# Spreading a block's recurrence, norm and queries over 122 slots, and its closing norm between the dots

## The reference

```
proj = h @ w_in                                  # 1024 -> conv group and RWKV-7 group
y_rw = RWKV-7 recurrence per head, group norm, + bonus, * gate
mix  = concat(y_cv, y_rw) @ w_o
h1   = layer_norm(ALPHA * h + mix)
q    = (h1 @ w_q)            # 8 heads x 2 halves x 128
sc   = q . sub_keys          # 16 times 128 scores a token
s_top, i_top = top_k(sc, 16)
best, pos = top_k(s_top0[:, None] + s_top1[None, :], 16)   # 16 of 256 pairs, per head
idx = i_top0 * 128 + i_top1 at pos;  gate = softmax(best)
hu  = peer_u[idx] . h1       # 128 rows of 1024 numbers for each token
out = sum(gelu(hu) * gate * peer_v[idx])
h2  = layer_norm(ALPHA * h1 + out)
```

## Time and profile before

| | |
|---|---|
| median of 3 runs | 3719.94 us (3712.74 to 3723.7) |
| the profiled execution | 3718.71 us, its span 3717.0 us |
| busy: PE, DVE, ACT, POOL | 3218.4, 2426.5, 801.9, 2105.5 us |
| granted TensorE clock, mean | 0.945 |
| DMA | 1239.85 MB |
| first dot of block 0 / block 1 / block 7 | at 672.08, 1058.31, 3297.66 us |

### The profile page before, as it was taken

How to read it: one execution, slowest core, us unless ns; L and a number is a source line. 1 busy time by engine, 2 the same in 40 slices (tenths; PEclk the granted TensorE clock), 3 DMA queues, 4 the chain that set the end, 5 groups by cost and what they waited for, 6 DMA issues and landing times.

```text
span 3717.0 us, 58838 instructions
## 1 busy us (share of the span) xinstructions
PE 3218.4 (87%) x17619; PEld 1706.6 (46%) x17619; DVE 2426.5 (65%) x5758; ACT 801.9 (22%) x1946; POOL 2105.5 (57%) x2172
## 2 busy tenths in 40 slices
PE   4996898599879987998799879987998799888977
PEld 3663565444534453445344534443444344442532
DVE  5463523867676767676766676667666766686795
ACT  2331000122122212221222122212221222121121
POOL 0012700377567756775677567756775677566575
PEclk9997999799999999999899989999999999999989
DMA  4344211899999999999999999999999999999997
GB/s 158 92 127 120 87 33 43 303 406 400 353 405 408 401 353 403 408 401 355 402 408 396 347 398 408 402 354 395 408 404 359 393 408 406 362 372 399 377 387 300
DMA packets 395698, 1239.85 MB, mean 334 GB/s; under 512 B 50834, under 2 KB 98326, under 8 KB 395216
## 3 DMA queue, kind: packets, MB, share of 16 engines
q0 software_dynamic: 302112, 1099.09, 76.4%
q1 hardware_dynamic: 91504, 134.41, 10.5%
q10 hardware_dynamic: 1728, 2.16, 0.2%
HBM read 1212.00 MB, written 31.94 MB: 335 GB/s over the span
## 4 chain that ended last, share of the span: by engine, by line
PE 58%; DVE 17%; issue 10%; DMA 4%; ACT 1%; DVEq 1%; POOL 0%; SPq 0%; ACTq 0%; POOLq 0%
PE ep_ps L1247 36%; PE front_ps L1116 9%; PE ep_ps L1293 5%; DVE rings L1630 4%; PE front_ps L1167 3%; PE front_ps L1185 3%; DMA rings<-in_peer_v_dram,idx 3%; DVE top_places L1544 1%; DVE top_places L1547 1%; DVE others L1545 1%; DMA rings<-in_peer_u_dram,idx 1%; DVE top_val L1546 1%; ACT diag L1366 1%; DVE top_idx L1548 1%; DVE top_val L1543 0%
## 5 line engine op out<-in xcount | busy, mean ns | idle before, releaser
L1247 PE MATMUL ep_ps<-rings,diag 128*128 128x512 f32 x4096 | 2027.6, 625 | 342.1 <-ACT diag L1366 296.1
L584 POOL DMA_INDIRECT rings<-in_peer_u_dram,idx x1024 | 985.3, 962 | 872.1 <-DVE hu L1630 318.0
L1630 DVE CUSTOM_DVE_ANT_0 rings<-rings,x_ps 128x1024 f32<-128x1024 f32 x1024 | 1237.4, 1212 | 89.8 <-DMA rings<-in_peer_u_dram,idx 54.3
L1247 PEld LDWEIGHTS ep_ps<-rings,diag 128*128 128x128 f32 x4096 | 736.9, 196 | 1110.7 <-issue 720.6
L584 POOL DMA_INDIRECT rings<-in_peer_v_dram,idx x1024 | 983.3, 960 | 386.8 <-issue 259.2
L1366 ACT ACTIVATE diag<-ident,act_v 128x128 f32<-128x128 f32 x1024 | 349.7, 391 | 262.0 <-PE ep_ps L1247 178.2
L1185 PEld LDWEIGHTS front_ps<-h1T,wq_ring 128*128 128x128 f32 x2304 | 284.1, 196 | 55.6 <-issue 54.9
L1185 PE MATMUL front_ps<-h1T,wq_ring 128*128 128x128 f32 (+1 forms) x2304 | 285.9, 276 | 1.2 <-issue 1.2
L348 PE MATMUL job_ps<-rings,w_ring 128*128 128x352 f32 (+2 forms) x672 | 208.7, 473 | 7.9 <-DMA w_ring<-in_w_in_dram 4.0
L1293 PE MATMUL ep_ps<-rings 128*128 128x352 f32 x576 | 197.2, 482 | 1.3 <-DMA rings<-in_w_in_dram 1.3
L1350 ACT ACTIVATE q_T<-front_ps 128x128 f32<-128x128 f32 (+1 forms) x144 | 38.4, 267 | 604.1 <-PE front_ps L1185 604.1
(11 more groups left out here) (349 smaller groups left out, 2903.8 us busy)
## 6 DMA issues: line engine op xcount, KB each, us to landing
wq_ring<-scratch_wq_tiles SPq DMA_DIRECT2D x144, 512.0 KB, 7.1
rings<-in_peer_u_dram,idx POOLq DMA_INDIRECT x1024
rings<-in_peer_v_dram,idx POOLq DMA_INDIRECT x1024
ops<-scratch_op_blocks SPq DMA_DIRECT2D x35, 256.0 KB
scratch_wq_tiles<-in_w_q_dram SPq DMA_DIRECT2D x16, 512.0 KB, 5.1
w_ring<-in_w_in_dram SPq DMA_DIRECT2D x12, 512.0 KB, 3.9
rings<-in_w_in_dram SPq DMA_DIRECT2D x12, 512.0 KB, 4.4
xrow<-in_x_prompt_dram SPq DMA_DIRECT2D x8, 512.0 KB, 3.7
```

What stands on the lines that cost most here:

```text
L584: return pool.indirect_dma_start(out=ring, out_offset=None, in_=table, in_offset=bass.IndirectOffsetOnAxis(ap=index, axis=0))
L1247: mm = pe.matmul(out_ps[:, half, :], diag[:, s % RING, :], v[:, s % RING, half * 512:(half + 1) * 512], start=head == 0 and s == 0, stop=h ...
L1630: dve.tensor_tensor_reduce(u[:, s % RING, :], u[:, s % RING, :], x, 1.0, 0.0, ALU.mult, ALU.add, hu[:, par, s:s + 1]).then_inc(dots, 1)
```

## The change

The front's steps get one running number f, and one table for all engines: 0 to 57 are the products, 58 (`NORM`) to 77 `norm_slot`, 78 the transposition, 80 to 118 the queries, and the last top 16 is at 121. In a block, step f stands in slot f, counted from slot 0 of turn 0. So the front begins in turn 0, no slot is left empty among the products, the norm's steps lie over 20 slots instead of 16 (the eight w_o steps at `MIX_AT`, with gaps), and the queries are 38 slots from first to last instead of 28. A query's scores still follow one slot later, its top 16 three slots later (`TOP_LAG`).

Block 1's front can't begin in turn 0 of block 0, since block 0's own ends there: it starts in turn 1 with two steps a slot, and from turn 2 on it is in place. The sample's front starts at `NORM` in turn 1 of the last block, over four turns instead of three; the sample's state moves to slot 0 of turn 0.

`finish` becomes six parts: the first, which reads `out_ps`, before the first dot of turn 1, the others after dots 1, 2, 4, 5 and 6 of that turn; ScalarE's root is in slot 3. The loop's body is now turns 2 to 7 and then turns 0 and 1 of the next block, run 6 times; the rest is written out before and behind. SP loads four tiles of w_q, then waits for the norm and loads the next block's operands, then the other twelve tiles. `rk` is awaited one step later on TensorE. Before the turns, where the convolution runs beside block 0's products, there are 87 slots instead of 93.

```diff
-        CONV_SLOTS = 92
+        CONV_SLOTS = 86
...
-        SCORE_SLOTS = [1 + (2 * TOPK - 4) * j // (HP - 1) for j in range(HP)]
-        assert SCORE_SLOTS[-1] + 1 < 2 * TOPK
+        NORM = 2 * len(PRODUCTS)
+        MIX_AT = (4, 5, 7, 8, 10, 11, 13, 14)
+        TURN_AT, H1T_AT, QUERY_AT = NORM + 20, NORM + 21, NORM + 22
+        QUERIES_OVER, TOP_LAG = 38, 3
+        SCORE_SLOTS = [QUERY_AT + QUERIES_OVER * j // (HP - 1) for j in range(HP)]
+        FRONT_END = SCORE_SLOTS[-1] + TOP_LAG + 1
...
+        def front_steps(turn, n, nb, s):
+
+            if nb is None:
+                return []
+            if rows_of(nb) == NS:
+                f = NORM + (n - 1) * TOPK + s
+                return [f] if n >= 1 and f < FRONT_END else []
+            if isinstance(turn, int) and turn == 1:
+                return [2 * s, 2 * s + 1]
+            return [n * TOPK + s]
 
         def over_turns(eng, a_turn, finish):
 
+            def rest_of_block(b, turn, nb):
+                for n in range(2, H):
+                    a_turn(turn + n, n, nb)
+
+            def start_of_block(b, turn, nb):
+                a_turn(turn, 0, nb, new_block=b)
+                a_turn(turn + 1, 1, nb, old_block=b - 1)
 
             a_turn(0, 0, None, sums=False)
-            with eng.Fori(0, TBLOCKS - 1) as b:
-                for n in range(1, H):
-                    a_turn(b * H + n, n, b + 1)
-                a_turn(b * H + H, 0, None, new_block=b + 1)
-                finish(b)
-            for n in range(1, H):
-                a_turn((TBLOCKS - 1) * H + n, n, TBLOCKS)
+            a_turn(1, 1, 1)
+            with eng.Fori(0, TBLOCKS - 2) as b:
+                rest_of_block(b, b * H, b + 1)
+                start_of_block(b + 1, b * H + H, b + 2)
+            b = TBLOCKS - 2
+            rest_of_block(b, b * H, b + 1)
+            start_of_block(b + 1, b * H + H, b + 2)
+            rest_of_block(b + 1, b * H + H, b + 2)
             a_turn(TBLOCKS * H, 0, None, dots_left=False)
             finish(TBLOCKS - 1)
...
             with sp.Fori(0, TBLOCKS - 2) as b:
-                load_wq(b + 1)
+                load_wq(b + 1, FIRST)
                 after_norm(b + 1)
                 load_block(b + 2)
+                load_wq(b + 1, LATER)
                 sp.wait_ge(x_taken, b + 2)
                 sp.sem_inc(waited_sp, 1)
                 load_h(b + 2)
                 store_y(b)
...
-                elif s - 4 < KT:
-                    kt = s - 4
+                elif s in MIX_AT:
+                    kt = MIX_AT.index(s)
...
-                    for j in queries(n, s, 1):
-                        top16(nb, j, rows)
+                for j in queries(f, TOP_LAG):
+                    top16(nb, j, rows)
...
+                if old_block is not None:
+                    finish(old_block, 0)
                 for s in range(TOPK):
                     dve.wait_ge(u_landed[s % RING], (turn * 2 + s // RING + 1) * 16)
                     dve.tensor_tensor_reduce(u[:, s % RING, :], u[:, s % RING, :], x, 1.0, 0.0, ALU.mult, ALU.add,
                                              hu[:, par, s:s + 1]).then_inc(dots, 1)
...
+                    for f in front_steps(turn, n, nb, s):
+                        front_slot(nb, f)
...
+                    if old_block is not None and s:
+                        finish(old_block, FINISH_AT.get(s))
                     if spread:
-                        pick_slot(turn, par, (n + 2) % H, s, SCORE_SLOTS[1] + 2 if n == 6 else 0)
+                        pick_slot(turn, par, (n + 2) % H, s)
...
+            FINISH_AT = {0: 0, 1: 1, 2: 2, 4: 3, 5: 4, 6: 5}
```

More of the change, by code:

```diff
@@ new lines, in ending, with rows_of @@
+        def ending(turn):
+            return isinstance(turn, int) and turn >= (TBLOCKS - 1) * H
+        def rows_of(nb):
+            return NS if isinstance(nb, int) and nb == TBLOCKS else P
+        def front_steps(turn, n, nb, s):
[7 more added lines that the diff above has]
+            return [n * TOPK + s]
@@ L802, in before_turns @@
                 n += 1
[L803 to L807, removed]
+            for f in range(NORM):
+                slot(0, f)
+                conv_slot(n)
+                n += 1
             assert n > CONV_SLOTS
@@ L1237, in a_turn @@
-            def a_turn(turn, n, nb, sums=True, dots_left=True, new_block=None):
+                    chunk_step(*chunk_slot(nb, f))
+                    return
+                if f == NORM and rows == NS:
+                    pe.wait_ge(ops_loaded, TBLOCKS * 112 + 160 + 32)
+                    pe.wait_ge(state_out, 1)
+                    pe.wait_ge(samp_copied, 5)
+                norm_slot(nb, f - NORM, rows)
+                if f == TURN_AT:
+                    turn_h1(nb, rows)
+                for j in queries(f, 1):
+                    key_scores(nb, j, rows)
@@ new lines, in front_slot, with sample_state @@
+                for j in queries(f):
+                    query(nb, j, rows)
+            def sample_state(nb):
+                pe.wait_ge(front_dve.sem, front_dve.value(nb, (f"top{HP - 1}", 1)))
+                for c in range(PAIRS):
+                    for head in range(2):
+                        r = slice(head * HD, (head + 1) * HD)
+                        last = pe.matmul(bank[0][r, c * HD:(c + 1) * HD], st[r, c, :], eye[r, :], start=True, stop=True)
+                last.then_inc(state_turned, 1)
+                pe.wait_ge(samp_chain, SAMP_STEPS)
+                pe.matmul(bank[1][:, 0:BH], samp_o[:, :, :].rearrange("p a b -> p (a b)"), t.ident[0:BH, 0:BH],
+                          start=True, stop=True).then_inc(samp_turned, 1)
@@ L1239, in a_turn @@
+            def a_turn(turn, n, nb, sums=True, dots_left=True, new_block=None, old_block=None):
                 head = (n - 1) % H
@@ L1580, in pick, with pick_slot @@
                 dve.sem_inc(picked, 1)
-            def pick_slot(turn, par, head, s, first):
-                done = lambda i: i * PICK_STEPS // (TOPK - first) if i > 0 else 0
-                for i in range(done(s - first), done(s + 1 - first)):
+            def pick_slot(turn, par, head, s):
+                for i in range(s * PICK_STEPS // TOPK, (s + 1) * PICK_STEPS // TOPK):
                     if i == 0:
@@ L1687, in _, with finish_last @@
+            def finish_last(b):
+                dve.tensor_scalar(res[:, :], x, ALPHA, None, ALU.mult).then_inc(block_chain, 1)
+                dve.wait_ge(block_chain, b * BLOCK_STEPS + 1)
+                for part in range(6):
+                    finish(b, part)
             done(dve.memset(st[:, :, :], 0.0), start_chain)
```

270 lines of the change are left out of this document (128 added, 142 removed).

## The result

| | before | after |
|---|---|---|
| median of 12 runs each | 3715.43 us (3710.96 to 3723.7) | 3708.38 us (3703.88 to 3712.13) |
| profiled span | 3717.0 us | 3710.4 us |
| granted clock, mean | 0.945 | 0.954 |

The ratio is 0.9978, with an interval of 0.997 to 0.9985. The change brings 7 us of the 71 that I had forecast, and the time lies 3 us above my range.

What follows compares the result with a forecast made beforehand. The DMA was taken to bound the kernel: 362 us a middle block against an engine chain of 355. Six blocks -67, first block +1, last -5 sum to -71 from 3719.9, so 3649 us; range 3602 to 3705.

Steps and rivals of the forecast that it cites:

- DMA by its share: Middle blocks: DMA engines keep a share of 1.03, so a block takes 362 us, 11.2 less than before.
- 20.6 us of reserve: Rings eight rows deep hold 16 gathers, 20.6 us of DMA, taken to carry the DMA through engine stalls.
- one region of 167 us: Recurrence's products with their turn ends: engine chain 167.4 us against 152 us of DMA, so the rings fill.
- The jump's size: Loop's edge between turns 1 and 2: copy, load and Gelu 2.0, edge 4.91, load 1.28, diagonal 0.4; 8.7 us.
- Between turns 0 and 1: TensorE stands only for the y sum on top of the slot 15 drain: 4 us, before 10.39.
- The slot 15 drains: At turn ends, slot 15's product is copied before table load and Gelu: 2.75 us, put at 3, or 2 in turn 2.
- The rival that made them the new bound: Turn ends except the loop's edge as long as 7.33 us: chain 388 us, kernel about 3825 us; slower, chance 0.08.
- the one of longer drains: Each of eight turn ends costs 1.4 us more: chain 366 us a block, kernel 3678 us; chance 0.23.
- Closing norm: Its other parts, about 5 us of VectorE between turn 1's dots, cost nothing; without idle time, 5 us a block.
- Queries and top 16: Queries over 42 slots: VectorE 116 us, TensorE 111; VectorE's 7.85 us wait for the first scores goes.
- First block: Turn 1 holds 32 products instead of 15, +18 us; turns 2 to 7 -17 us; together +1.
- The signs of being wrong: Turn-end TensorE idle over 45 us a block, query turns' share under 1.0, or VectorE waiting for products in turns 0-3.

## Why the prediction was wrong

The failed step is one sentence: "So stalls of 9 us do not starve the DMA for long, and I take the DMA by its share: 362 us". I had the jump's move, and its size nearly right; I then costed it at nothing, covered by "20.6 us of reserve". Without any jump the kernel takes 361.8 us a block and 3642 us in all, against forecasts of 362 and 3649. The miss is 59 us. The step explains it whole: 5 x 12.9 = 64.5 us in blocks 1 to 5, nearly all of the 66 us between the kernels with and without the loop, and everything else together came out 7 us better than forecast. In part that 362 is met by luck: I took the DMA at its full share throughout, and turns 1 and 4 fall short of it (386 and 382 GB/s).

Why the reserve was not there. I counted from the trace how many gathers are open, that is, issued on GpSimd and not yet landed by their packets. The rows are turns of the third block and the columns are the starts of slots 0, 2, 4 and so on to 14:

```
kernel after          0    2    4    6    8   10   12   14
turn 1              7.1  3.7  1.7  1.5  2.0  3.7  3.7  6.1
turn 2 (jump ahead) 5.6  3.4  1.4  2.2  2.7  3.6  2.8  3.2
turn 3              2.8  2.5  2.6  1.8  2.3  1.9  1.3  2.0
turn 4              3.2  1.0  2.0  2.2  2.8  3.4  4.1  4.2
turn 6              9.5  9.6  7.9  7.8  9.0 10.2  8.8  9.8
without a loop
turn 1              6.5  3.2  1.5  2.6  1.8  3.5  3.3  5.7
turn 2              7.4  7.0  5.1  5.2  5.3  5.2  5.3  5.6
turn 3              5.3  4.9  5.0  4.2  4.3  3.9  2.5  2.4
turn 4              3.3  1.8  2.0  2.2  2.6  2.5  3.5  3.6
kernel before
turn 0              3.7  1.4  3.0  2.7  2.8  3.5  3.5  3.5
```

Sixteen buffers are never sixteen gathers in flight: at no time in these three kernels are more than 12.4 open. In the full turns 5 to 7 of the kernel after it is 5 to 10; the other buffers hold rows that wait for their dot or sum, or are free and not yet asked for. When the last gather ahead of the jump is issued, about 8 are open, 10 us of transfers at 2.57 us for two. From 1524 to 1534 us one gather is issued while the engines carry on at 396 GB/s, and the count goes from 7.2 to 0.7; that is where the row of 248 GB/s begins. So the stall eats the whole reserve once.

What I had not asked is what refills it. In turn 2 and most of turn 3 a product stands in every slot, TensorE is as slow as the transfers, and the count stays between 1 and 4 once the first slots are over, where without a jump it is 5 to 7 in turn 2 and 4 to 5 in most of turn 3: the reserve is gone for these two turns, and small waits in them cost transfers. Turns 1 and 4 are as low without a jump. I had one region of 167 us whose 152 us of DMA "fill" the rings; but they are filled in the light turns 5 to 7, and behind a stall in the product turns they are not. Behind turn 6, where 9 to 12 are open and light turns follow, the same jump costs 4.7 us.

The windows show the hole in turns 2 and 3, and the experiments show that the jump is its cause; that the open gathers explain the price by place is argued from these counts, as no kernel changed the depth of the rings. The count alone does not order the prices either. In the kernel before only 3.5 gathers are open at its jump, and it costs 5.5 us: there the nine gathers that GpSimd still had to issue fed the DMA engines. And behind turn 0 of the kernel after about 7 are open, but the jump costs 10 to 11 us: in the third block GpSimd itself stands 9.9 us there with "issue" as the releaser, and turn 1 runs at 338 GB/s. So, by these rows, the reserve at a stall is the open gathers and the free buffers that GpSimd can still fill, as long as it is not stalled as well.

The other steps:

- *The jump's size.* 8.7 us forecast (4.91 on ScalarE, a second table load, a diagonal), 11.12 measured. The second table load was not there: the timeline goes from the idle 8.71 straight to the diagonal. ScalarE's idle time alone was 8.71 instead of the 4.91 of the earlier trace rows. It is a mis-sized term: 2.4 us too little.
- *Between turns 0 and 1.* Forecast 4 us; the timeline of the kernel after has 3.65:

```profile
1473.12 1.86 ACT L1393 ACTIVATE diag<-ident,act_v 128x128 f32<-128x128 f32 x6 [0.38 <-DVE act_v L1688]
...
1474.42 3.36 PE L1271 MATMUL ep_ps<-rings,diag 128*128 128x512 f32 x4 [3.65 <-ACT diag L1393]
```

- *The slot 15 drains.* Forecast 2.75 us, measured 2.81 at the end of turn 1 of the kernel without a loop. The rival that made them the new bound, and the one of longer drains, are out. The second was named beside a rule of the Trainium skill (ScalarE: Activation LUTs, What ACT_TABLE_LOAD costs: 1.28 us and a drain of 1.38). The load is 1.28 us here again, and no drain shows between it and Gelu, which starts 0.01 us after its end:

```profile
1518.86 1.28 ACT L1420 ACT_TABLE_LOAD   x1
1520.15 0.21 ACT L1420 ACTIVATE act_v<-hu 128x16 f32<-128x16 f32 x1
```

- *Closing norm.* Right in kind; 14 and 16 us measured with and without the jump's stall, over a third of what the spread front is worth.
- *Queries and top 16.* The wait for scores went as forecast, from 7.85 us to at most 0.8. The wait for the w_o product, which I had go or shrink, stayed. Waits of VectorE in turns 4 to 7 of the kernel after (total us, times, longest):

```profile
DVE rings L1666 <- DMA rings<-in_peer_u_dram,idx: 8.5, 12, 1.6
...
DVE h_block L1556 <- PE front_ps L1193: 5.7, 1, 5.7
...
DVE top_val L1576 <- PE front_ps L1220: 1.6, 3, 0.8
```

  It was 4.73 in the earlier trace rows and is 5.7 now. The gaps between the w_o steps are not what it hangs on: in the third block without a loop it is 6.2 us with the gaps and 6.0 with the steps in a row, so my reason for it (TensorE's work in eight slots on end) does not hold. Spreading the queries gains nothing (3642.06 against 3642.11) and spreading the w_o steps at most a few us. In the query turns the DMA is full either way (408 to 409 GB/s); in turn 4, with most of the norm, it is not (382 and 379 GB/s), and what bounds that turn was not found.
- *First block.* 53.6 (its terms add up to 53.1) and 272 us forecast for turn 1 and turns 2 to 7; 52.6 and 271.8 measured. Without a loop the two are 319.3 us together, 5 less, so the close match may be luck.
- *Last block.* Turns 1 to 4 were forecast at 195 us; they are 198.0, only 1 below. Its turn 0 took 42.4 us instead of 37.4, which I had not reckoned with: the sample's state moved into it. Whether that is the cause was not tried.
- *DMA by its share.* Turns with a share of 1.03 stayed at 406 to 409 GB/s, in the kernels with and without a loop. The Trainium skill (HBM Reference, Specifications) has about 425 for a core that streams alone, which by my estimate would have given 3608 us; no full turn here came near that rate.
- *The signs of being wrong.* None of the three would have caught this. TensorE's waits for a diagonal at turn ends add up to 20 us in the third block, far from 45. The query turns are full. And VectorE waited for products within turns 0 to 3 in the kernel before already (up to 3.2 us at a time), so that sign could not tell the two cases apart.

What stays open. About 44 us lie between the two schedules without jumps: some 16 are the closing norm, a few may be `TOP_LAG` and `MIX_AT`, none are the queries. The rest, the recurrence from turn 0 on and the norm over 20 slots, was not taken apart. I also did not find why ScalarE's idle time at a jump is 8.71 us behind turn 1 and 3.90 behind turn 6 while VectorE's is 5.55 in both (third block), nor whether block 0's 5 us are the loop's.

The best kernel of the study has the new schedule and no loop: 3642 us, 2% below the kernel before. With a loop, the jump behind turn 6 gives 3669, 1.2% below.

## What to carry to other kernels

A hardware loop's jump stalls several engines at once (here VectorE, ScalarE and with them TensorE), so it is an operation with a place in the schedule. When a change moves it, price it where it lands, by a run with the jump moved or the loop written out. Here it was cheapest where most transfers were in flight and the engines had slack behind it, and no jump at all was cheapest. And count the reserve of a prefetching ring as transfers in flight at that moment, from the trace, and those that can still be issued, instead of as buffers, and ask what refills it. In the product turns here nothing did, and the two costs added where I had taken the larger of two sums.

## What I had not expected of the hardware

- One jump back is 5.55 us of idle time on VectorE and 3.90 to 8.71 on ScalarE in the third block of the kernels above; in the kernel before VectorE stands 4.67 us and ScalarE 4.91. The Trainium skill (Advanced Engine Details and Errata, Control Flow Timing) gives some 51 ns for a branch and 108 ns for a compare and branch; the branch itself is thus a small part of what a loop costs here. The trace shows one thing that crowds at jumps: transfers of the kind that the DMA view calls instruction. In the 14 us from 1520 on of the kernel after, that view has (packets, MB, share of 16 engines)

```profile
q14 instruction: 8, 0.07, 1.5%
q8 instruction: 2, 0.03, 1.0%
```

  where a stretch of the same length at that turn's end without a loop, from 1500 to 1514, has

```profile
q8 instruction: 1, 0.02, 0.5%
```

  There are 10 such packets at each of the five jumps of the kernel after, 7 or 8 at those of the kernel before, and never more than 5 within 13 us away from a jump. Five of the ten come between 1521.5 and 1524.1 us, and VectorE goes on at 1526.19. That they bring the code behind the jump and that the engines wait for it is likely by their times, and no run shows it.
- In the stretch from 1524 to 1534 us, of which TensorE stood idle for the first 5.5 us, the granted clock is 0.50, the lower level, 1.2 GHz. The first four matmuls of 512 columns took 3.78 us together (the timeline with the jump, above), the next four 2.45 and the four after them 1.98 (TensorE's timeline, below). So the stall of 11 us is followed by about 2 us more.

```profile
1534.29 2.45 PE L1271 MATMUL ep_ps<-rings,diag 128*128 128x512 f32 x4
1537.29 1.98 PE L1271 MATMUL ep_ps<-rings,diag 128*128 128x512 f32 x4
```

- With the jump behind turn 6 the first sum is as slow (3.78 us) after only 5.27 us of standing, and that jump is still the cheapest of the four places.
